# Latent projections of a hybrid attention and recurrence block: query weights and second latents loaded during the recurrence, query products moved ahead of the second key and value products

## What is computed

```python
(c_q, c_kv, k_pe, gate_a, hq, hf, hi, gate_b, merge_logits) = jnp.split(proj, split_at, axis=-1)
q = (rmsnorm(c_q, g_q[l]) @ w_uq[l]).reshape(b, s, MLA_HEADS, MLA_QK)
q_nope, q_pe = q[..., :MLA_NOPE], apply_rope(q[..., MLA_NOPE:], cos, sin)
kv = (rmsnorm(c_kv, g_kv[l]) @ w_ukv[l]).reshape(b, s, MLA_HEADS, MLA_NOPE + MLA_V)
k_nope, v = kv[..., :MLA_NOPE], kv[..., MLA_NOPE:]
```

## Time and profile before

| what | value |
|---|---|
| median of 3 runs | 2247.88 us (2238.98 to 2257.52) |
| profiled execution, device time | 2249.32 us |
| its span in the profile | 2247.5 us |
| PE busy over the span | 2119.2 us, 94% |
| DVE, ACT busy | 1364.3 us (61%), 1033.7 us (46%) |
| mean granted clock of PE | 0.976 |
| latent projections, first product to Q 3's end | about 1120.5 to 1309 us |

### The profile page before, as it was taken

How to read it: one execution, slowest core, us unless ns; L and a number is a source line. 1 busy time by engine, 2 the same in 40 slices (tenths; PEclk the granted TensorE clock), 3 DMA queues, 4 the chain that set the end, 5 groups by cost and what they waited for, 6 DMA issues and landing times.

```text
span 2247.5 us, 34185 instructions
## 1 busy us (share of the span) xinstructions
PE 2119.2 (94%) x12181; PEld 1797.7 (80%) x12181; DVE 1364.3 (61%) x2191; ACT 1033.7 (46%) x1854; POOL 425.1 (19%) x380
## 2 busy tenths in 40 slices
PE   7999999999999899999879889999999998999998
PEld 5799878878998678888757667887788876778886
DVE  6633445475335457877656657776777767565652
ACT  5322335433214446666542336665656665344441
POOL 3322222453212222233223400000000040000000
PEclk9999999999999979999989989999999999999999
DMA  5432335334324233333287852133331238474651
GB/s 145 130 104 69 106 96 179 101 100 127 113 66 145 71 90 100 106 112 112 89 298 237 267 144 49 34 73 74 72 75 33 49 104 266 140 224 149 187 159 66
DMA packets 264392, 273.16 MB, mean 122 GB/s; under 512 B 38609, under 2 KB 194705, under 8 KB 261777
## 3 DMA queue, kind: packets, MB, share of 16 engines
q1 hardware_dynamic: 253776, 252.36, 38.7%
q0 software_dynamic: 5696, 10.79, 1.8%
q10 hardware_dynamic: 4800, 8.42, 1.0%
HBM read 178.16 MB, written 93.35 MB: 121 GB/s over the span
## 4 chain that ended last, share of the span: by engine, by line
PE 46%; DMA 5%; DVE 4%; ACT 4%; issue 3%; SPq 1%; POOL 1%; ACTq 0%; DVEq 0%; POOLq 0%
PE bankE L74 4%; PE bankE L76 4%; PE bankE L75 4%; PE scores L74 3%; PE bankD L74 3%; PE turn_rest L2650 3%; PE scores L75 3%; PE scores L76 3%; PE bankD L76 3%; PE bankD L75 3%; PE o_acc L2662 2%; PE o_acc L2663 2%; DMA e_g_in<-gateTok 2%; PE turn_first L2650 2%; ACT probs L2464 1%
## 5 line engine op out<-in xcount | busy, mean ns | idle before, releaser
L2444 DVE TENSOR_REDUCE small_chunk_min<-scores 128x1 f32<-128x512 f32 (+2 forms) x320 | 181.6, 605 | 41.2 <-PE scores L76 26.4
L865 DVE TENSOR_TENSOR shared_w_lo<-shared_w_raw,shared_w_hi 128x512 fp32r<-128x512 f32 x138 | 109.5, 796 | 137.7 <-ACT shared_w_hi L666 137.6
L2464 ACT ACTIVATE probs<-scores,small_least 128x1024 f32<-128x1024 f32 (+2 forms) x192 | 167.2, 871 | 15.0 <-DVE small_least L2451 13.4
L2598 DVE TENSOR_TENSOR pT<-turn_rest,pT 128x512 fp32r<-128x512 f32 (+2 forms) x208 | 126.2, 625 | 53.3 <-ACT pT L2564 53.3
L666 ACT ACTIVATE shared_w_hi<-shared_w_raw 128x512 fp32r<-128x512 f32 x138 | 84.4, 625 | 152.8 <-POOL shared_w_raw L541 71.9
L74 PE MATMUL scores<-k_sb,q_sb 96*128 96x512 f32 (+2 forms) x320 | 129.3, 404 | 20.2 <-ACT probs L2464 15.0
L2564 ACT ACTIVATE pT<-turn_rest 128x512 fp32r<-128x512 f32 (+2 forms) x208 | 109.7, 549 | 74.4 <-PE turn_rest L2650 59.1
L1082 PE MATMUL bankA<-sums_hi,shared_w_hi 128*128 128x512 f32 x336 | 132.5, 394 | 2.4 <-DVE outs L911 1.7
L1082 PE MATMUL bankA<-sums_hi,shared_w_lo 128*128 128x512 f32 x336 | 131.0, 390 | 0.0
L1082 PE MATMUL bankA<-sums_lo,shared_w_hi 128*128 128x512 f32 x336 | 130.8, 389 | 0.0
L2662 PE MATMUL o_acc<-pT,v_sb 128*128 128x512 f32 (+1 forms) x320 | 125.1, 395 | 4.8 <-DVE pT L2598 3.9
...
## 6 DMA issues: line engine op xcount, KB each, us to landing
shared_w_raw<-in_w_in_dram SPq DMA_DIRECT2D x96, 256.0 KB, 3.0
projT<-outs SPq DMA_DIRECT2D x96, 256.0 KB, 2.4
e_l_in<-projT SPq DMA_DIRECT2D x64, 256.0 KB, 5.0
...
projT<-d_stage ACTq DMA_DIRECT2D x32, 256.0 KB, 3.0
knT<-b_out SPq DMA_DIRECT2D x32, 256.0 KB, 3.5
vTok<-b_out SPq DMA_DIRECT2D x32, 256.0 KB, 4.0
```

Of the source, the lines that this page charges most:

```text
L865: dve.tensor_tensor(slot_lo(u, i), operand(u, i), slot_hi(u, i).bitcast(F32), ALU.subtract).then_inc(w_ready, 1)
L2444: dve.tensor_reduce(chunk_min[:, i % 2, c:c + 1], scores[:, s_bank(i, c), 0:width(i, c)], AX.X, ALU.min)\
L2464: act.activation(probs[b][:, r, first * BLK:first * BLK + n], src, ACT.Exp, bias=least[:, i % 2:i % 2 + 1], scale=-1.0, accum_out=sums[:, ...
L2598: dve.tensor_tensor(pT[:, at % RING, 1, r0 * P:], turn[TURN_AT[tile] % TURN_RING][:, r0 * P:], pT[:, at % RING, 0, r0 * P:].bitcast(F32), ...
```

## The change

Four things change.

1. In the recurrence stage SP issues four loads before the last 4 units, behind the loop: w_uq in two pieces (`wq_rest`, 1536 KB; `wq_two`, 768 KB), the latents of KV 1 (`next_latents`, 512 KB), and the query gain (3 KB). They go to memory that neither the recurrence nor the start of the next stage uses; paddings place them there. The latent stage no longer loads them, and issues the load of Q 0's latents second, right behind one row of scales.
2. The block order has Q 0 before KV 1.
3. The query weight pieces are prepared in another order, first the 6 large ones, then the 12 for the X outputs. PE waits for each large piece on its own in Q 0's first output, and for all pieces only before its first X output.
4. The jobs beside the outputs are laid out anew (`BESIDE`): Q 0's latents and the large pieces beside KV 0, the X pieces at the end of KV 0 and in Q 0's first two outputs. Some waits follow: POOL's loads of the shared key and ACT's first work on Q 1's latents wait for all weight pieces; the load of KV 2's latents moves to the start of Q 0, that of KV 3's to KV 2.

The diff, cut to its core:

```diff
+    def beside_early(self, nc, ctx):
+        sb("pad0", [P, 896])
+        self.wq_two = sb("wq_two", [P, 2, HEADS * QK])
+        sb("pad1", [P, P * TPB])
+        self.next_latents = sb("next_latents", [P, KKV, BLK])
...
                     for blk in range(NB):
                         unit(pair, blk, pair * NB + blk)
+                w_uq_v = w_uq.rearrange("(k p) n -> p k n", p=P)
+                sp.dma_start(own.wq_rest[:], w_uq_v[:, 2:]).then_inc(next_in, 16)
+                sp.dma_start(own.wq_two[:], w_uq_v[:, 0:2]).then_inc(next_in, 16)
+                sp.dma_start(own.next_latents[:], projT[KQ:N_LORA, :, BLK:2 * BLK].rearrange("k p n -> p k n")).then_inc(next_in, 16)
+                sp.dma_start(own.q_gain[:], g_q.rearrange("o (k p) -> p (o k)", p=P), allow_slow_non_contiguous=True).then_inc(next_in, 16)
                 for blk in range(NB - 1):
                     unit(PAIRS - 1, blk, (PAIRS - 1) * NB + blk, True)
...
-    BLOCKS = ((KV, 0), (KV, 1), (Q, 0), (KV, 2), (Q, 1), (KV, 3), (Q, 2), (Q, 3))
+    BLOCKS = ((KV, 0), (Q, 0), (KV, 1), (KV, 2), (Q, 1), (KV, 3), (Q, 2), (Q, 3))
...
+        W_PARTS = KV_PARTS + Q_PARTS + X_PARTS
...
+        beside(KV, 0, 0, ("w", 0), ("w", 1))
+        for i in range(4):
+            beside(KV, 0, 1 + i, ("w", 2 + i), ("c", Q, 0, i))
+        beside(KV, 0, 5, ("c", Q, 0, 4), ("c", Q, 0, 5))
+        beside(KV, 0, 6, ("w", 6), ("w", 7), ("w", 8))
+        beside(KV, 0, 7, ("w", 9), ("w", 10), ("w", 11))
+        beside(Q, 0, 0, ("w", 12), ("w", 13), ("w", 14))
+        beside(Q, 0, 1, ("w", 15), ("w", 16), ("w", 17))
+        beside(Q, 0, 2, ("c", KV, 1, 0), ("c", KV, 1, 1))
         for i in range(2):
+            beside(Q, 0, 3 + i, ("c", KV, 2, i))
         for i in range(3):
+            beside(KV, 1, 1 + i, ("c", Q, 1, i))
+            beside(KV, 2, i, ("c", Q, 1, 3 + i))
...
             load_rs(0, KV)
-            sp.dma_start(gain[:, 0:KQ], g_q.rearrange("o (k p) -> p (o k)", p=P),
-                         allow_slow_non_contiguous=True).then_inc(wq_in, 16)
+            load_c(0, Q)
             sp.dma_start(rstd[:], rsTok).then_inc(const_in, 16)
             sp.dma_start(ident[:], ident_d).then_inc(const_in, 16)
-            load_c(1, KV)
-            sp.dma_start(wq_raw[:], w_uq.rearrange("(k p) n -> p k n", p=P)).then_inc(wq_in, 16)
-            load_c(0, Q)
+            load_rs(1, KV)
...
             load_cs(0)
-            pool.wait_ge(prod_done, products_of(KV, 1))
+            pool.wait_ge(w_ready, len(W_PARTS))
             load_k()
...
+                if (g, blk) == (Q, 1):
+                    act.wait_ge(w_ready, len(W_PARTS))
...
-                        if (g, blk) == (Q, 0):
-                            pe.wait_ge(w_ready, N_WKV + N_WQ)
+                    if (g, blk, i) == (Q, 0, X_AT):
+                        pe.wait_ge(w_ready, N_WKV + N_WQ)
...
+                        if (g, blk, i) == (Q, 0, 0):
+                            pe.wait_ge(w_ready, N_WKV + k + 1)
```

More of the change, by code:

```diff
@@ L1227, in stored_from @@
         self.o_out = ctx.enter_context(nc.sbuf_tensor("d_o_out", [P, TPB, 2, VD], F32))
+        ctx.enter_context(nc.sbuf_tensor("d_pad2", [P, BLK], F32))
+        self.q_gain = ctx.enter_context(nc.sbuf_tensor("d_q_gain", [P, KQ], F32))
 class Small:
@@ L1246, in __init__, with merge_logits_and_recurrence @@
         self.inv = sb("inv", [P, TPB])
-def merge_logits_and_recurrence(nc, hT_hi, hT_lo, shared, early, own, w_in, projT, hgTok, oB, w_ukv, g_kv):
+def merge_logits_and_recurrence(nc, hT_hi, hT_lo, shared, early, own, w_in, projT, hgTok, oB, w_ukv, g_kv, w_uq, g_q):
     UNITS = PAIRS * NB
@@ L1785, with latent_projections @@
 PE_ROWS, ROT_ROWS = slice(NOPE, QK), slice(QK, P)
-def latent_projections(nc, small, shared, projT, rsRow, rsTok, g_q, w_uq, rope_d, ident_d, qnT, qpT, knT, kpT, vTok):
+def latent_projections(nc, small, shared, own, projT, rsRow, rsTok, rope_d, ident_d, qnT, qpT, knT, kpT, vTok):
     V_AT, KV_EV = PAIRS, PAIRS + TPB
@@ L1838, in latent_projections @@
         ident = small.ident
-        gain = sb("gain", [P, N_LORA])
+        sb("gain", [P, N_LORA])
         rstd = sb("rstd", [P, TT])
@@ L1884, in latent_projections, with raw_query_weights @@
         wkv_v = wkv_raw.rearrange("p k (h n) -> p k h n", n=P)
-        wq_v = wq_raw[:].rearrange("p k (h n) -> p k h n", n=QK)
         def per_head(ap, n):
             return ap.rearrange("p (h n) -> p h n", n=n)
+        def raw_query_weights(k):
+            raw = own.wq_two[:, k] if k < 2 else own.wq_rest[:, k - 2]
+            return raw.rearrange("p (h n) -> p h n", n=QK)
         def gain_of(k):
-            return gain[:, k:k + 1] if k < KQ else shared.kv_gain[:, k - KQ:k - KQ + 1]
+            return own.q_gain[:, k:k + 1] if k < KQ else shared.kv_gain[:, k - KQ:k - KQ + 1]
         def raw_latents(g, blk, m):
-            return shared.kv_latents[:, m] if (g, blk) == (KV, 0) else c_lo[blk % 2][:, TILES[g][m]].bitcast(F32)
-        KV_PARTS = [(hi[:, k], lo[:, k], wkv_v[:, k, :, n0:n0 + NOPE], NOPE, KQ + k)
+            if g == KV and blk < 2:
+                return (shared.kv_latents, own.next_latents)[blk][:, m]
+            return c_lo[blk % 2][:, TILES[g][m]].bitcast(F32)
+        KV_PARTS = [(per_head(hi[:, k], NOPE), per_head(lo[:, k], NOPE), wkv_v[:, k, :, n0:n0 + NOPE], KQ + k)
                     for hi, lo, n0 in ((wk_hi, wk_lo, 0), (wv_hi, wv_lo, NOPE)) for k in range(KKV)]
-        Q_PARTS = [(wq_hi[:, k, to:to + HEADS * n], wq_lo[:, k, to:to + HEADS * n], wq_v[:, k, :, of:of + n], n, k)
-                   for k in range(KQ) for to, of, n in ((0, 0, NOPE), (X1, NOPE, HALF_ROPE), (X2, NOPE + HALF_ROPE, HALF_ROPE))]
-        W_PARTS = KV_PARTS + Q_PARTS
+        Q_PARTS = [(per_head(wq_hi[:, k, 0:W], NOPE), per_head(wq_lo[:, k, 0:W], NOPE), raw_query_weights(k)[:, :, 0:NOPE], k)
+                   for k in range(KQ)]
+        X_PARTS = [(per_head(wq_hi[:, k, to:to + P], HALF_ROPE), per_head(wq_lo[:, k, to:to + P], HALF_ROPE),
+                    raw_query_weights(k)[:, :, of:of + HALF_ROPE], k)
+                   for k in range(KQ) for to, of in ((X1, NOPE), (X2, NOPE + HALF_ROPE))]
+        W_PARTS = KV_PARTS + Q_PARTS + X_PARTS
         KEY_TURNS = ((KV, 2, 0), (Q, 1, 0))
@@ L2099, in scalar @@
                         else:
-                            if job[1] == 0:
-                                act.wait_ge(wq_in, 32)
                             round_weights(N_WKV + job[1])
```

52 lines of the change are left out of this document (23 added, 29 removed).

## The result

| | kernel before | changed kernel |
|---|---|---|
| median | 2241.57 us (2236.23 to 2257.52, 7 runs) | 2231.70 us (2228.51 to 2235.17, 7 runs) |
| profiled execution, span | 2247.5 us | 2226.8 us |
| mean granted clock | 0.976 | 0.979 |

The ratio is 0.9934, with a 95% interval of 0.991 to 0.9958: of 2241.57 us that is 14.8 us less, between 9.4 and 20.2 (the two medians in the table lie 9.9 us apart). Two repetitions of the changed kernel beside other runs gave 0.9942 (0.9921 to 0.9963) and 0.9934 (0.9909 to 0.9958). The forecast was 12 us less.

A forecast was written before the change was run, and what follows sets the result against it. PE bounds the recurrence; the latent projections lose 19.9 us to late weights and stores. These go, 5.0 come back in Q 0 and 2.8 in KV 1 and KV 2: 12 us less, median 2236 us, range 2224 to 2249.

The forecast's parts named there:

- The loads beside the recurrence: Four early loads, 2.8 MB, in the recurrence: cost 0, their delay staying inside unit 14's slack; bounds 0 and 7 us.
- the rival with unit 14: Recurrence: unit 14's values or gates come late and PE waits; held for 35 us it costs 12, 2250 us; chance 0.02.
- KV 0: First block of the latent stage: first product stays at 1120.5 us and the block ends at 1133.3, 12.8 us as before.
- Q 0: Query block now after KV 0: 24.6 us of matmuls plus 5.0 lost, ending at 1163; bounds 1158 and 1171.
- the microsecond for a lower clock: In Q 0: 1 us added for the clock falling to 0.83 and 0.90 in stretches with holes.
- KV 1 and KV 2: Two key-value blocks now in a row, bounded by DVE and ACT: 28.5 us, against 21.8 by PE's own pace.
- the rival of the store ring: 16 outputs in a row wait for store buffers; decides from 10.4 us landing, at 14.5 gives 2258 us; chance 0.05.
- The upper bound of 31.2 us: For KV 1 and KV 2: 14.8 + 16.4 us, if each takes as long as KV 2 and KV 3 did.
- The holes: PE's 19.9 us lost between KV 0's and Q 0's ends before the change, put down to late weights and stores.
- The waits from there on are local and hang on events that move along: Behind KV 1 and KV 2: order is the old one, so Q 1's start moving from 1203.66 to 1191.5 us carries through.
- Part of it only: Gain 0 to 8 us, middle 2243: Q 0's latents land late or KV 1 and KV 2 take 31.2; chance 0.17.
- More: Gain 16 to 24 us, 2228: Q 0 doesn't wait and KV 1 with KV 2 runs nearer PE's 21.8; chance 0.12.

The follow-up runs named there:

- e8_copies: Changed kernel plus five transfers of 2304 KB, copying the query weights to unread memory, behind the early loads; 2258.41 us, beside 2242.04 for the kernel before.
- e5_split: Changed kernel with Q 0's latents loaded in two transfers with a signal each; 2225.3 us in one run.
- e6_key: Changed kernel with the rotary key's shares moved from KV 2 and Q 1 to Q 1 and Q 2, cosines loaded before the key's store; 2231.35 us.
- e1_loads: Changed kernel with the old block order, jobs and waits, so only the loads beside the recurrence remain; ratio 0.9944 to the kernel before.
- e2_order: Changed kernel with the new order and jobs, but weights and KV 1's latents loaded in the latent stage as before; ratio 0.9982 to the kernel before.

## Why the prediction was right

The forecast was 12 us less for the whole program, 14.8 with an interval of 9.4 to 20.2 was measured. By its steps:

- **The loads beside the recurrence.** Taken at 0, measured at 0 (86.48 against 86.50 us). The working held too: 11.7 us of extra delay estimated, 14.1 - 3.5 = 10.6 measured for the values, inside the slack of 22.8. One term in it was wrong and cost nothing: SP's issues were taken at 0.4 us each, and three behind the big loads took 4.00, 1.73 and 3.88 us. The trace of before had such an issue, of 6.39 us, so this could have been read beforehand. The bound of 7 us for this part doesn't follow from its own numbers either: three times 11.7 us less 22.8 of slack is 12.3, the 12 us that the rival with unit 14 has. `e8_copies` shows what lies beyond the slack.
- **KV 0** stayed, 12.46 us against 12.8.
- **Q 0.** Forecast 24.6 + 5.0 = 29.6 us, measured 31.95, 31.62 and 31.66. The waits on the tiles' pace were 4.0 in the forecast and are 1.24 + 2.33 + 0.90 = 4.5, in the two other profiles 3.7 and 3.8. Undersized was the microsecond for a lower clock: the stretch has 0.89, and 24.6 / 0.89 = 27.6, three microseconds; PE's busy time there is 27.5, 27.9 and 27.8 us. What was known to be at 0.83 to 0.90 in such stretches should have gone into the sum as it stood. The latents landed 11.4 us after issue, not 7.3; that was 4 us off, of which `e5_split` gives back at most 0.9.
- **KV 1 and KV 2** were forecast at 28.5 us, measured at 28.24 to 28.25. The walk along DVE's reads was right in the term that mattered: `e6_key` takes the shared key out and the pair loses 3.1 us, which is the prediction's 5.7 less an ordinary round of 2.57. PE's pace (21.8) and the rival of the store ring were both off: with stores landing in 2.8 us the ring isn't the bound. The upper bound of 31.2 us was read wrongly: 1229.32 is the row of a wait inside KV 3, whose first matmul is at 1228.28, so KV 3 took 17.5 us and not 16.4, and the bound would be 32.3.
- **The holes.** The prediction puts all 19.9 us of them down to the late weights and the late stores. `e1_loads`, without either, still has 5.71 us ahead of Q 0; that one was ACT's and DVE's work, and it was the new order, with its jobs, that removed it.
- **"The waits from there on are local and hang on events that move along"** is the step that failed. The cosines' wait hangs on which of two queues issues first, and that changed by a microsecond. It gave 2.1 to 2.8 us. The two errors, 2.4 us too little in Q 0 and 2.8 us too little behind Q 1, nearly cancel: at Q 1 the gain was 10.5 where 12.2 had been forecast, at the last product 12.7. That the end came so close to 12 is luck to that extent.
- **The rivals.** "Part of it only" had its cause in the late latents, and these were late, but not by enough. "Slower: unit 14" is a real mechanism with its edge, by the estimate beside `e8_copies`, at about twice the volume of this change. "More" did not come.

So the size of the gain at Q 1 was right by its mechanism, within two microseconds at each block's start: 19.9 us of loss gone, and 7.35 in Q 0 and 2.4 in the pair come back, some 10 where the forecast had 5.0 and 2.8. `e1_loads` and `e2_order` show that in stage time two thirds to three quarters of it is the loads, and that the order is worth its 3 us at Q 1 only with them.
